# The indexer's transposes one slot sooner in a software-pipelined step, and vector's split ahead of the close

## The chip, the cores and the metric

The kernel runs on one core of one Trainium2 chip. A core has five engines that run their own instruction streams and meet at semaphores: TensorE (PE in the profile, matrix products and transposes), VectorE (DVE), ScalarE (ACT), GpSimd (POOL) and SyncE (SP, which issues the DMA transfers). The metric is the device time of one execution in microseconds (us), as the median of several.

## What is computed

One layer of a hybrid encoder: 4096 new frames of a prompt (32 tiles of 128 rows) and 128 frames of eight running streams (tile 32). Cut to what bears on the change:

```python
h = rms_norm(x, norm_g)
p = h @ w_in                  # q, k, v, gate of two head groups, and the indexer's qi, ki, wi
# group A: attention in a sliding window;  group B: for each query the 256 best keys
r = relu(einsum('bqhe,ble->bqhl', qi, ki_all))        # 4 heads of 64, all keys so far
score = einsum('bqhl,bqh->bql', r, wi)
_, idx = lax.top_k(score, 256)
# attention over those keys, gates silu(ga), silu(gb), then y @ w_out + x
```

The kernel has three stages. The first, which the change touches, projects every tile, normalizes, stores q, k, v and gates, scores each tile against all keys so far (the indexer), and finds the 256th largest score of each row by a search of 32 counting tests. The second does the attention, the last the output projection and the sample frames.

## The kernel before

Stage one is a loop over steps t = 0 to 33, each of 12 slots. In step t PE projects tile t group by group: `kv` at slot 0, `qa` at 2, `qb` at 4, `idx` at 6, and from step 10 on the gates `ga` at 8 and `gb` at 10. From step 23 on two more gates, those of the tiles 0 to 9 that were left out, follow at slots 9 and 11. PE also transposes the next tile's x (slots 5 and 7), the indexer's query and key of tile t (slot 9, `transpose_indexer`, L578 and L581 of the profile), and computes the scores of tile t-1 (L614), spread over slots 0 to 7. Each engine's stream is in program order, written out by such slots.

ACT evacuates what PE projects (L700 for most groups and, as `ring`, for gates, L698 for `idx`), copies the transposes (L722 for the indexer's query, L725 for its key, L670 for x), applies relu to the scores (L737), which POOL weighs and adds (L908 to L913). Between these ACT runs the search of even tiles (tests at L807). DVE runs the search of odd tiles (tests at L1043), squares for the norms (L946, L950), the split of the indexer's query and key into a high and a low part (L956, L961), and the close of every search (`choose`, L969 to L980; for ACT's tiles it starts at L989). A planner decides where this extra work stands between the tests: it adds up fixed costs (`dve_us`, `act_us`, `test_us`, `close_us`) and puts each piece in when its planned time `us_at(t, slot)` is reached. It orders, it does not time.

The search of a pair of tiles takes two steps. ACT's search ends in an odd step, so DVE's close of it stands in an odd step near slots 9 to 11; in most of the odd steps it stood ahead of the split. PE's first score product of the next step waits for both parts of the split (semaphore `s_lo`). The transposes use two PSUM banks in turn: the one of the indexer's key (L581) waits until ACT has copied the second half of the next x (L670, one slot after the evacuation of `idx`).

Of the kernel before, what the change touches and what calls it, by code (L numbers as in the profile page):

```python
# [23 lines left out]
P = 128  # L24
# [7 lines left out]
HD = 64  # L32
# [94 lines left out]
SLOTS = 12  # L127
RELU_GAP = 1.8
BIG = float(2 ** 100)
TESTS = 32  # L130
# [80 lines left out]
def dve_us(t, slot):  # L211

    return 3.4 * (slot == 6) + 1.2 * (slot == 11) if t <= TILES else 0.0

# [69 lines left out]
def stage_one(nc, x_prompt, x_sample, norm_g, w_in, q_norm_a, k_norm_a, q_norm_b, k_norm_b,  # L284
# [3 lines left out]
    with ExitStack() as ctx:  # L288
# [94 lines left out]
        def _(sp):  # L383
# [67 lines left out]
            for t in range(TILES + 2):  # L451
# [36 lines left out]
                else:  # L488
                    sp.dma_start(b_kidx_sample[0].rearrange("b t d -> (b t) d"), proj[:, PKI:PKI + HD]).then_inc(s_ki, 16)
                chosen_until(us_at(t, 9))  # L490
                if t >= LATER:
                    sp.wait_ge(s_ev, PROJ["ga", t] + 1)
                    from_ring(gates[t, :, 0:STEP])
                if e is not None:
                    sp.wait_ge(s_ev, PROJ["ga", e] + 1)
                    from_ring(gates[e, :, 0:STEP])
                if t == TILES:
                    sp.wait_ge(s_tc, PIECE["iq", t] + 1)
                    from_ring(qi_new, HD)
                    sp.wait_ge(s_tc, PIECE["ik", t] + 1)  # L500
                    from_ring(ki_new, HD, P)
                sp.wait_ge(s_kn, t + 1)
# [33 lines left out]
        def _(pe):  # L536
# [63 lines left out]
            def score_units(u, slot):  # L600

                for j, (c, n) in enumerate(units(u)):
                    if unit_slot(u, j) != slot:
                        continue
                    if j == 0:
                        pe.wait_ge(s_lo, 2 * u + 2)
                    for h in range(IDX_HEADS):
                        at = SCORED[u] + IDX_HEADS * j + h
                        if at >= 4:
                            pe.wait_ge(s_rl, at - 3)  # L610
                        if at == 0:
                            pe.wait_ge(s_rampc, 1)
                        for part in range(2):
                            ins = pe.matmul(s_bank[at % 4][:, 0:n], qi[:, part, h * P:(h + 1) * P], kiT[:, c:c + n],  # L614
                                            start=(part == 0), stop=(part == 1))
                        ins.then_inc(s_s, 1)
# [3 lines left out]
            for t in range(TILES + 2):  # L620
                for slot in range(SLOTS):
# [10 lines left out]
                    if slot in (5, 7) and t < TILES:  # L632
                        transpose_x((slot - 5) // 2, t + 1)
                    if slot == 9 and t <= TILES:
                        transpose_indexer(t)
# [5 lines left out]
        def _(act):  # L641
# [97 lines left out]
            def background():  # L739
# [5 lines left out]
                for t in range(TILES + 3):  # L745
                    for slot in range(SLOTS):
                        before, b = divmod(SLOTS * t + slot - 1, SLOTS)
                        yield us_at(t, slot)
                        if b == 0 and 1 <= before <= TILES + 1:
                            copy_piece("k", before - 1)  # L750
                        for at, name, of in groups_of_step(before) if 0 <= before <= TILES else ():
                            if at == b:
                                evacuate(name, of)
# [6 lines left out]
                        if slot == 4 and t < TILES:  # L760
                            square_x(t + 1)
                        if b == 9 and before <= TILES:
                            copy_piece("iq", before)
                            copy_piece("ik", before)
                        if 3 <= t <= TILES:
# [164 lines left out]
        def _(dve):  # L930
# [73 lines left out]
            def background():  # L1004

                taken = 2
                for t in range(TILES + 5):
                    for slot in (0, 3, 6, 9, 11):
                        while taken < SEARCHED and FOUND_AT[taken] <= us_at(t, slot):
                            yield FOUND_AT[taken]  # L1010
                            choose_act(taken)
                            taken += 2
                        if slot == 6 and t <= TILES:
                            yield us_at(t, slot)
                            sum_heads(t)
                        if slot == 11 and t < TILES:
                            yield us_at(t, 10.3)
                            split_q(t)
                            split_k(t)
# [1514 lines left out]
```

## Time and profile before

| | us |
|---|---|
| median of 3 runs (5093.58 to 5100.38) | 5097.78 |
| the profiled execution | 5096.76 |
| its span, first to last instruction | 5095.0 |

| engine | busy us | share of the span |
|---|---|---|
| PE | 4347.4 | 85% |
| DVE | 3499.8 | 69% |
| ACT | 3443.3 | 68% |
| POOL | 1619.9 | 32% |

The times of the trace count from the span's start. Stage one ends, and the next stage's first instructions run, at 2456 us. A wait in these views is written as engine, what it was about to write, its line, and the instruction that ended the wait. The PE clock of a stretch is given as a share of 2.4 GHz.

### The profile page before, as it was taken

Reading aid. Unit: us, or ns where it says so; the run is one execution under the profiler, and the core shown is the slowest. Engines: PE = TensorE matmul, PEld = TensorE weight load, DVE = VectorE, ACT = ScalarE, POOL = GpSimd, SP = SyncE. Lnnn points to the kernel's source line nnn. Section 1 sums busy time; section 2 is a strip of 40 time slices with the busy share of each in tenths; the row PEclk is TensorE's granted clock in tenths of the full one; section 3 lists DMA queues with packets and bytes.
Section 4 is the critical chain, followed back from the end, with each engine's and each line's share of the span. In section 5 each row is a group of like instructions: output and inputs, shape, how many; then the busy total and the mean of one; then the engine's idle time right before and its main releaser. Section 6 shows DMA issues by size and latency. Waiting matters only on the chain. (4 is left out here: it accounts for less than half of the span.)

```text
span 5095.0 us, 78325 instructions
## 1 busy us (share of the span) xinstructions
PE 4347.4 (85%) x26505; PEld 2718.1 (53%) x26505; DVE 3499.8 (69%) x6644; ACT 3443.3 (68%) x6887; POOL 1619.9 (32%) x1358
## 2 busy tenths in 40 slices
PE   6777888777677786767689999989999999989999
PEld 3344444434343343434366777767777777754444
DVE  1277779888797898989477777787777778625111
ACT  1588888888787798872488888858788885520100
POOL 1345566667557757777210000000000000000000
PEclk8888889888788898978799999999999999999999
DMA  5211111100010111101421111011010010044422
GB/s 143 70 44 45 38 39 40 37 35 28 33 42 33 37 45 38 36 32 48 157 72 58 44 51 40 28 54 41 25 42 25 28 40 26 10 126 132 117 93 103
DMA packets 201975, 276.98 MB, mean 54 GB/s; under 512 B 50496, under 2 KB 134176, under 8 KB 201056
## 3 DMA queue, kind: packets, MB, share of 16 engines
q1 hardware_dynamic: 198624, 271.81, 16.9%
q8 instruction: 220, 3.60, 0.3%
q14 instruction: 171, 1.40, 0.1%
q10 hardware_dynamic: 2960, 0.17, 0.0%
HBM read 156.73 MB, written 114.16 MB: 53 GB/s over the span
## 5 line engine op out<-in xcount | busy, mean ns | idle before, releaser
L596 PE MATMUL bank<-w,x 128*128 128x512 f32 (+1 forms) x2848 | 1258.6, 598 | 19.2 <-DVE w L941 12.8
L1043 DVE TENSOR_SCALAR_CACHE_REDUCE ties<-score,cand 128x512 int8<-128x512 f32 (+13 forms) x448 | 1110.6, 2479 | 122.1 <-POOL score L917 106.7
L596 PEld LDWEIGHTS bank<-w,x 128*128 128x128 f32 x2848 | 576.9, 206 | 608.6 <-issue 549.7
L807 ACT ACTIVATE act_junk<-score,a_cand,a_sign 128x384 int8<-128x384 f32 (+13 forms) x420 | 879.4, 2094 | 14.0
L614 PE MATMUL bank<-kiT,qi 128*128 128x512 f32 (+3 forms) x1136 | 396.5, 489 | 450.5 <-ACT relu L737 244.9
L1834 DVE CUSTOM_DVE_ANT_0 row<-bank,mask 128x512 f32<-128x512 f32 (+3 forms) x1024 | 622.6, 639 | 181.6 <-PE bank L1573 180.3
L1540 POOL TENSOR_TENSOR near_bias<-table,mask 128x2048 f32<-128x2048 f32 (+1 forms) x32 | 129.5, 4047 | 1767.8 <-DVE part L1834 1751.4
L1768 ACT ACTIVATE pT<-bank 128x512 f32<-128x512 f32 (+2 forms) x704 | 368.4, 523 | 428.5 <-PE bank L1589 426.6
L1670 ACT ACTIVATE row<-row,top 128x1024 f32<-128x1024 f32 (+7 forms) x640 | 632.9, 990 | 4.0 <-DVE top L1847 4.0
L1573 PE MATMUL bank<-kT,qb 64*128 64x256 f32 (+1 forms) x4352 | 609.6, 397 | 9.0 <-DVE part L1834 5.6
L1589 PE MATMUL bank<-ident,row 128*128 128x128 f32 x4224 | 594.6, 281 | 26.4 <-DVE pT L1945 19.6
L1945 DVE COPY pT<-bank 128x512 f32<-128x512 f32 (+2 forms) x704 | 425.2, 604 | 255.8 <-PE bank L1589 254.2
L1618 PE MATMUL bank<-pT,v 128*64 128x128 f32 x8448 | 590.0, 280 | 0.0
L913 POOL TENSOR_TENSOR score<-score,relu 128x512 f32<-128x512 f32 (+3 forms) x426 | 560.3, 1315 | 33.4
L614 PEld LDWEIGHTS bank<-kiT,qi 128*128 128x128 f32 x1136 | 237.6, 232 | 578.3 <-ACT relu L737 307.0
L1618 PEld LDWEIGHTS bank<-pT,v 128*64 128x64 f32 x8448 | 450.9, 137 | 171.1 <-issue 163.7
L910 POOL TENSOR_TENSOR relu<-relu,weight 128x512 f32<-128x512 f32 (+3 forms) x426 | 499.3, 1172 | 76.9 <-ACT relu L737 76.7
L1589 PEld LDWEIGHTS bank<-ident,row 128*128 128x128 f32 x4224 | 453.1, 141 | 132.2 <-issue 97.0
L737 ACT ACTIVATE relu<-bank 128x512 f32<-128x512 f32 (+3 forms) x568 | 297.7, 554 | 252.1 <-POOL score L913 177.0
L2290 PE MATMUL bank<-wo,mix_in 128*128 128x512 f32 x1024 | 450.9, 599 | 0.0
L1573 PEld LDWEIGHTS bank<-kT,qb 64*128 64x128 f32 x4352 | 380.3, 187 | 125.5 <-issue 72.1
L908 POOL TENSOR_TENSOR score<-relu,weight 128x512 f32<-128x512 f32 (+3 forms) x142 | 164.6, 1159 | 651.4 <-issue 527.9
(255 smaller groups left out, 4900.1 us busy)
## 6 DMA issues: line engine op xcount, KB each, us to landing
qk_t<-ring SPq DMA_DIRECT2D x66, 256.0 KB, 2.0
gates<-ring SPq DMA_DIRECT2D x66, 256.0 KB, 2.0
gate<-gates SPq DMA_DIRECT2D x33, 512.0 KB, 3.4
out<-x_in SPq DMA_DIRECT2D x33, 512.0 KB, 2.9
x<-in_x_prompt SPq DMA_DIRECT2D x32, 512.0 KB, 3.7
mixed<-mixT SPq DMA_DIRECT2D x64, 256.0 KB, 2.0
mix_in<-mixed SPq DMA_DIRECT2D x32, 512.0 KB, 4.3
x_in<-in_x_prompt SPq DMA_DIRECT2D x32, 512.0 KB, 3.8
```

The costliest lines, as they stand in the source:

```text
L596: ins = pe.matmul(p_bank[n % 2][:, 0:n1 - n0], held[:, c * P:(c + 1) * P], w[:, c, n0:n1], start=(c == 0), stop=(c == KC - 1))
L614: ins = pe.matmul(s_bank[at % 4][:, 0:n], qi[:, part, h * P:(h + 1) * P], kiT[:, c:c + n], start=(part == 0), stop=(part == 1))
L807: tick(act.activation(junk, row, ACT.Sign, bias=c, scale=back, accum_out=a_sum[:, :]))
L910: k = tick(pool.tensor_tensor(r, r, weighs, ALU.mult))
L913: pool.tensor_tensor(to, to, r, ALU.add).then_inc(s_pa, 1)
L1043: n = tick(dve.tensor_scalar(ties[:, 0:width], row, c.bitcast(F32), 0.0, ALU.is_ge, ALU.add, accum_out=counts[:, i:i + 1]))
L1573: ins = pe.matmul(s[:, h * STEP + c0:h * STEP + c0 + m], qb[t % 2][half, g, :], kT[half, c + c0:c + c0 + m], start=True, stop=True)
L1589: ins = pe.transpose(t_bank[h][:, b * P:(b + 1) * P], held, ident[:, :])
L1618: ins = pe.matmul(oT[0 if k < 2 else 1][half * HD:(half + 1) * HD, col:col + P], value, pT[h][at % 2][:, b * P:(b + 1) * P], start=first, ...
L1670: act.activation(at, at, ACT.Exp, bias=bias, accum_out=out).then_inc(s_exp, 1)
L1834: ins = dve.tensor_tensor_reduce(row[k % 2][:, h, c0:c0 + w0], s[:, h * STEP + c0 - c:h * STEP + c0 - c + w0], more, 1.0, PAD, ALU.add, AL ...
L2290: ins = pe.matmul(y_bank[k % 2], held, w[:, c, i * STEP:(i + 1) * STEP], start=(c == 0), stop=(c == KC - 1))
```

## The change

Five edits in stage one. PE's `transpose_indexer` stands at slot 8 instead of 9, and so ahead of the first gate's projection. ACT's copies of the two transposes follow one slot sooner, ahead of its evacuation of the first gate. DVE's split is planned at slot 9.3 instead of 10.3, and the planner no longer puts the close of an ACT tile at slot 9 but at 7 or 11, so that no close stands between slot 9 and the split. PE's first score product waits for the query's part of the split alone, and only the last one (whose keys hold the new tile) for the key's. SP's stores of the sample tile's query and key follow the new order once, in step 32.

```diff
+SPLIT = 9.3
 def dve_us(t, slot):
-    return 3.4 * (slot == 6) + 1.2 * (slot == 11) if t <= TILES else 0.0
+    return 3.4 * (slot == 6) + 1.2 * (slot == 9) if t <= TILES else 0.0
...
                     if j == 0:
+                        pe.wait_ge(s_lo, 2 * u + 1)
+                    if j == len(units(u)) - 1:
                         pe.wait_ge(s_lo, 2 * u + 2)
...
-                    if slot == 9 and t <= TILES:
+                    if slot == 8 and t <= TILES:
                         transpose_indexer(t)
...
+                        if b == 8 and 0 <= before <= TILES:
+                            copy_piece("iq", before)
+                            copy_piece("ik", before)
                         for at, name, of in groups_of_step(before) if 0 <= before <= TILES else ():
                             if at == b:
                                 evacuate(name, of)
...
-                        if b == 9 and before <= TILES:
-                            copy_piece("iq", before)
-                            copy_piece("ik", before)
...
-                    for slot in (0, 3, 6, 9, 11):
-                        while taken < SEARCHED and FOUND_AT[taken] <= us_at(t, slot):
+                    for slot in (0, 3, 6, 7, SPLIT, 11):
+                        while slot != SPLIT and taken < SEARCHED and FOUND_AT[taken] <= us_at(t, slot):
...
-                        if slot == 11 and t < TILES:
-                            yield us_at(t, 10.3)
+                        if slot == SPLIT and t < TILES:
+                            yield us_at(t, SPLIT)
                             split_q(t)
                             split_k(t)
```

PE's instructions at the end of step 21 of the kernel before, from the last score product of tile 20 to the first projection of step 22 (bank is PSUM, a projection is 8 products here):

```order
L614 MATMUL bank<-kiT,qi 128x128 x8
L596 MATMUL bank<-w,x 128x324 x8
L557 MATMUL bank<-ident,x 128x128 x4
L596 MATMUL bank<-w,x 128x512 x8
L578 MATMUL bank<-ident,proj 128x128 x4
L581 MATMUL bank<-ident,proj 128x128
L596 MATMUL bank<-w,x 128x512 x8
L614 MATMUL bank<-kiT,qi 128x512 x8
```

The same place in the changed kernel, whose lines stand one to three further down:

```order
L617 MATMUL bank<-kiT,qi 128x128 x8
L597 MATMUL bank<-w,x 128x324 x8
L558 MATMUL bank<-ident,x 128x128 x4
L579 MATMUL bank<-ident,proj 128x128 x4
L582 MATMUL bank<-ident,proj 128x128
L597 MATMUL bank<-w,x 128x512 x16
L617 MATMUL bank<-kiT,qi 128x512 x8
```

The five transposes of the indexer stood between the two gates and now stand ahead of both. PE's stream changes so in each of the 23 steps that have gates; before step 10 it does not change.

DVE's instructions at the end of step 21 before, around the close of tile 18 (score is its row of scores, ties and mask are results):

```order
L1043 TENSOR_SCALAR ties,counts<-score,cand 128x2560
L989 TENSOR_SCALAR pick<-a_found 128x1
L991 SCALAR_TENSOR_TENSOR pick<-a_found,pick 128x1
L993 TENSOR_SCALAR ties,pick<-score,pick 128x2432
...
L972 SCALAR_TENSOR_TENSOR score<-ties 128x2432
L975 SCALAR_TENSOR_TENSOR pick<-score,pick 128x1
L977 SCALAR_TENSOR_TENSOR ties<-score,pick,ties 128x2432
L980 SCALAR_TENSOR_TENSOR mask<-ties,mask 128x2432
L956 TENSOR_TENSOR qi<-bank,qi 128x512
L961 TENSOR_TENSOR kiT<-bank,kiT 64x128
```

The same place in the changed kernel:

```order
L1046 TENSOR_SCALAR ties,counts<-score,cand 128x2560
L959 TENSOR_TENSOR qi<-bank,qi 128x512
L964 TENSOR_TENSOR kiT<-bank,kiT 64x128
L1050 TENSOR_SCALAR flag<-counts 128x1
L1053 TENSOR_SCALAR cand<-flag,cand 128x1
L1046 TENSOR_SCALAR ties,counts<-score,cand 128x2560
L992 TENSOR_SCALAR pick<-a_found 128x1
```

The split moved from behind the close to ahead of it, over one test too. It passes a close in steps 9, 17, 19, 21, 23, 25, 27, 29 and 31, and two to four tests of a search in most others.

## Rows read from the trace of the kernel before

**Rows 1.** Busy time by stretch: steps 4 to 21, and 22 to 30

```profile
core 0: us, PE busy (x) PEld busy (x) DVE busy (x) ACT busy (x) POOL busy (x), PEclk, DMA share, GB/s
187.00:1330.00 1143.00, 868.18 (x2506) 469.23 (x2507) 900.17 (x1414) 974.03 (x1919) 675.08 (x580) 0.86 0.11 39
1330.00:2300.00 970.00, 727.74 (x1922) 380.80 (x1921) 838.93 (x736) 801.00 (x1125) 660.95 (x535) 0.85 0.11 37
```

**Rows 2.** Waits of PE, ACT, DVE, 187 to 1330 us: total, times, longest

```profile
PE bank L614 <- DVE kiT L961: 183.0, 19, 22.1
...
ACT proj L700 <- PE bank L596: 59.3, 27, 6.3
...
ACT relu L737 <- PE bank L614: 6.9, 6, 3.3
...
DVE ties L946 <- ACT proj L700: 115.0, 10, 26.0
DVE ties L1043 <- POOL score L917: 45.7, 7, 12.0
```

**Rows 3.** Waits of PE and DVE, 1330 to 2300 us

```profile
PE bank L614 <- DVE kiT L961: 7.0, 3, 3.8
...
DVE ties L1043 <- POOL score L917: 61.0, 5, 15.9
DVE ties L946 <- ACT proj L700: 42.8, 5, 12.9
```

**Rows 4.** Timeline at the end of step 21: start, length, instruction, idle before

```profile
1273.13 7.03 PE L596 MATMUL bank<-w,x 128*128 128x512 f32 x16
...
1281.95 7.03 PE L596 MATMUL bank<-w,x 128*128 128x512 f32 x16
1311.06 3.60 PE L614 MATMUL bank<-kiT,qi 128*128 128x512 f32 x8 [22.07 <-DVE kiT L961]
...
1292.33 2.75 DVE L993 TENSOR_SCALAR_CACHE_REDUCE ties<-score,pick 128x2432 int8<-128x2432 f32 x1
...
1288.87 0.67 ACT L700 ACTIVATE ring<-bank,row_scale 128x512 f32<-128x512 f32 x1
...
1312.31 0.60 ACT L737 ACTIVATE relu<-bank 128x512 f32<-128x512 f32 x1 [2.61 <-PE bank L614]
...
1321.86 0.69 ACT L700 ACTIVATE proj<-bank,row_scale 128x512 f32<-128x512 f32 x1 [6.30 <-PE bank L596]
```

**Rows 5.** Timeline at the end of step 22

```profile
1390.09 0.48 PE L581 MATMUL bank<-ident,proj 128*128 128x128 f32 x1 [6.62 <-ACT x L670]
...
1393.30 0.67 ACT L700 ACTIVATE ring<-bank,row_scale 128x512 f32<-128x512 f32 x1
```

**Rows 6.** Timeline at the end of step 26, four gates

```profile
1757.18 7.03 PE L596 MATMUL bank<-w,x 128*128 128x512 f32 x16
...
1781.42 0.48 PE L581 MATMUL bank<-ident,proj 128*128 128x128 f32 x1 [7.01 <-ACT x L670]
1781.69 8.86 PE L596 MATMUL bank<-w,x_later 128*128 128x512 f32 x16
...
1803.72 2.41 PE L614 MATMUL bank<-kiT,qi 128*128 128x512 f32 x8
...
1806.64 0.66 ACT L700 ACTIVATE ring<-bank,row_scale 128x512 f32<-128x512 f32 x1
```

**Rows 7.** Timeline in step 25: DVE's close begins, ACT's first gate

```profile
1667.68 0.21 DVE L989 TENSOR_SCALAR pick<-a_found 128x1 f32<-128x1 f32 x1
...
1675.24 0.67 ACT L700 ACTIVATE ring<-bank,row_scale 128x512 f32<-128x512 f32 x1
```

**Rows 8.** Timeline in the middle of step 22

```profile
1352.52 2.17 DVE L946 TENSOR_TENSOR ties<-proj 128x1280 f32<-128x1280 f32 x1 [12.93 <-ACT proj L700]
...
1361.61 6.22 POOL L908 TENSOR_TENSOR score<-relu,weight 128x512 f32<-128x512 f32 x1
```

**Rows 9.** Timeline at the end of step 31

```profile
2341.91 3.59 PE L614 MATMUL bank<-kiT,qi 128*128 128x512 f32 x8 [13.48 <-DVE kiT L961]
```

**Rows 10.** Busy time and PE clock in PE's wait of step 21

```profile
1290.00:1311.00 21.00, 0.00 (x0) 0.00 (x0) 20.27 (x18) 19.11 (x29) 0.00 (x0) 0.59 0.18 62
```

More of the change, by code:

```diff
@@ L490, in _ @@
                 chosen_until(us_at(t, 9))
+                if t == TILES:
+                    sp.wait_ge(s_tc, PIECE["iq", t] + 1)
+                    from_ring(qi_new, HD)
+                    sp.wait_ge(s_tc, PIECE["ik", t] + 1)
+                    from_ring(ki_new, HD, P)
                 if t >= LATER:
@@ L496, in _ @@
                     from_ring(gates[e, :, 0:STEP])
[L497 to L501, printed above, removed]
                 sp.wait_ge(s_kn, t + 1)
```

## The prediction

> **What bounds the kernel now.** I read the busy time by stretch first. Stage one ends at 2456 us of a span of 5095, and no edit touches what follows. In steps 4 to 21 ACT is busy 974 of 1143 us, DVE 900 and PE 868 [rows 1]: no engine is full, so the streams hold each other up. The waits say where. In that stretch PE waits 183.0 us in 19 places, once a step, for DVE's split ahead of the first score product. ACT waits for PE only 59.3 us at projections and 6.9 at relus; DVE waits 115.0 for the evacuation that feeds its squares and 45.7 for finished scores [rows 2]. After step 21 PE's wait for the split is gone, 7.0 us in nine steps, since four gates keep it busy, while DVE still idles 61.0 and 42.8 [rows 3]. The timeline of step 21 shows the mechanism: DVE closes ACT's tile from 1292 us on, the split comes behind the close, and PE, done with its gates at 1289.0, idles 22.07 until 1311.06. ACT reaches the first relu at 1309.7 and waits 2.61 there and 6.30 at the next projection [rows 4]. ACT's later evacuation releases DVE in step 22 after 12.93 of idling [rows 8]. So the loop runs DVE's close, split, PE, ACT, DVE, and of PE's long wait only ACT's part reaches it.
>
> **The change part by part.** No product, copy or test is added or removed; five transposes on PE, two copies on ACT and two subtractions on DVE move per step.
>
> *The split ahead of the close (gain).* At step 21 ACT's copies take the place of its gate evacuation, 1288.87 instead of about 1293. DVE stands at a test's end at 1288.5 (one test ahead of its close at about 1292), so the split is done near 1291. PE has two gates to do behind the transposes: those can't end before ACT has copied x, 1281.8, so the gates end at 1282.1 + 2 x 7.03 = 1296.2. The scores begin there, 14.9 sooner, and ACT, at 1309.7, waits for nothing: it gets back 2.61 + 6.30 = 8.9, not 22. I sum it by ACT's waits, not PE's. They are 59.3 + 6.9 = 66.2 for steps 4 to 21 [rows 2]; going through the timeline, 42 of them stand behind a split, at the first relu and the first projections, and the rest at later projections, where PE has again waited for ACT. Bounds: 8.9, the one step shown, and 66.2. I take **-42**. What hides a lateness of the split now is that ACT gets there 15 us later; should the close still come first somewhere, the step is as before.
>
> *The transposes ahead of the first gate (loss).* Before, PE did a gate while ACT evacuated `idx` and copied x. Now it waits. In step 26 the gate that ran at 1757.18 for 7.03 must follow the key's transpose, which waits for ACT until 1781.42. Four gates from 1781.9 (7.03 + 8.86 + 7.03 + 7.03) end at 1811.8 instead of 1804.2, 7.6 later. ACT's last gate evacuation stood at 1806.64 and now waits 5.1, with its search behind it [rows 6]. In step 22 the first gate ends at 1390.6 + 7.0 = 1397.6, and ACT, which comes from 1393.30 and 0.8 of copies, waits 3.5 [rows 5]. Behind the waiting ACT stand its tests, the next evacuations and relus, so POOL too. The other even steps of 10 to 20 give 0.3 to 3.3 by the same reckoning, 12 for the seven with step 22; steps 24, 26 and 28 give about 5 each, 15; in the odd steps ACT arrives after the gates' new end and the price is about nothing, hidden by its tests. Sum **+27**. Bounds: nothing, where ACT's own waits for POOL absorb it, and 7.6 in each of the 23 gate steps.
>
> *DVE ahead of ACT.* In step 25 DVE reaches the split at 1667.68, but ACT copies the query only where its first gate stood, 1675.24 [rows 7]. DVE will wait about 8 us there in front of its close, and 6 or so in 23, 27 and 29: 27 us in all. I cost it at nothing, since the next even step has DVE idling, 61.0 + 42.8 us in five steps [rows 3], and it ends those steps by ACT's and POOL's time. Without that cover it costs the 27.
>
> *The end.* In step 31 PE waits 13.48 for the split until 2341.91 [rows 9]. It was ready at 2328.4; with the first gate 7.4 later it is ready at 2335.8, and nothing waits behind it but evacuations: **-5** of the 6.1. The weaker wait at the first score product saves the key's subtraction, 0.3 a step, nothing where PE comes after it. SP's two stores change places once, with work around them: nothing.
>
> Sum: -42 + 27 - 5 = -20. Against the profiled execution, 5096.8 (its span plus 1.8), that is 5077; the median of the runs shown is 1.0 above it, so **5078**.
>
> PE's clock: while PE idled from 1290 to 1311 its granted clock was 0.59 on average, so it fell to the lower level, 1.2 GHz; the gate that followed a pause in step 26 took 8.86 against 7.03 [rows 6, 10]. The Trainium skill ("TensorE: Matmul & The Clock Gate", Part 1) says the same of an idle PE, and it speaks against new pauses ahead of a gate. By it and these rows, six odd steps with a new pause lose 1.8 each, 11 in all, and the sum would be -9, 5089, if no slack took it; by the rows of step 21 alone, where ACT comes 13 us after PE, it is -20. I keep -20.
>
> **The rivals.**
>
> *PE's whole gain is passed on.* At step 21 PE gains 14.9 where ACT gains 8.9. If POOL and the relus behind start as much earlier as PE does, the 42 grows by that ratio to 70, and the sum is -70 + 27 - 5: 5050. For it: DVE has 160.7 us of idling to give in these steps [rows 2]. Against: ACT's relus stand at planned places between tests, and it doesn't idle there. Chance 0.16.
>
> *The gain is given back on the way.* ACT comes sooner to the same relus, but POOL adds no faster under DVE's closes: at 1361.61 one product took 6.22 us under DVE's scan [rows 8]. If half of the 42 ends so, -21 + 27 - 5 = +1: 5099. The change then does in effect nothing. Chance 0.22. The Trainium skill ("SBUF — State Buffer", Who interferes with whom) has GpSimd and VectorE share a pair of ports by an exclusive lock; the 6.22 agrees. By that rule each close that now meets additions stops them, and this rival gains; at step 21 the close would end at about 1309, just before ACT's relu, so it would stop none.
>
> *Slower: PE's pause ahead of the first gate runs through.* If ACT has no slack, an even step of 10 to 22 loses 3.5 (as 22 does) and one of 23 to 30 loses 5 (as 26 does): 24 + 40 = 64 against 47 gained, +17: 5115. It decides from 47 us on, 3.1 a step over these fifteen. For it: in steps 23 to 30 PE had no wait for the split left to win, so only the loss is there. Against: in odd steps ACT comes late. Chance 0.20.
>
> **How the numbers follow.** My forecast, -20 with its own range 5063 to 5089, gets 0.42. 0.2% is 10 us, about what can be told from no change here. Faster by more: the forecast's 0.42 and the first rival's 0.16, so 0.58; same 0.22; slower 0.20. The range leaves out about half of each outer rival: 5045 to 5112. It holds the bounds of the loss at 0 (5051) and most of the gain's.
>
> **What would show it.** Right: PE's waits for the split in steps 3 to 21 fall from 183 to under 50, and ACT's waits for PE at the first projections with them, by some 40; new waits appear on PE at the transposes of the indexer and ACT gets waits at `ring`; DVE gets waits of 6 to 8 us at the split in steps 23 to 29 and idles less in even steps. Steps 4 to 21 take 30 to 40 us less, steps 22 to 30 are 10 to 20 longer. Wrong: if steps 4 to 21 shrink by as much as PE's waits, ACT's plan was no limit; if the later steps grow by over 40, the pause runs through; if DVE's wait at the split lengthens odd steps, its idling was no cover.

## The result and the profile after

The changed kernel takes 5119.80 us (median of 5 runs, 5116.71 to 5121.0) against 5094.48 for the kernel before on the same chip: ratio 1.0049, 95% interval 1.0037 to 1.0061, 25 us slower. The forecast was 5078 and its range ended at 5112. The kernel before took between 5094.5 and 5095.5 on each of the chips used below, so the medians of the runs can be compared with each other. The profiled execution's span is 5114.9 us.

Busy time by stretch, answering to [rows 1]: core, stretch, then busy us of PE, PEld, DVE, ACT and POOL, the granted clock, DMA.

```profile
core 0: us, PE busy (x) PEld busy (x) DVE busy (x) ACT busy (x) POOL busy (x), PEclk, DMA share, GB/s
187.00:1330.00 1143.00, 895.03 (x2506) 476.12 (x2504) 888.38 (x1402) 973.35 (x1914) 679.99 (x577) 0.87 0.11 39
1330.00:2300.00 970.00, 704.88 (x1867) 370.01 (x1866) 814.33 (x726) 784.14 (x1102) 637.12 (x515) 0.83 0.11 37
```

Up to 1330 us ACT and POOL have done what they had before; from 1330 to 2300 every engine does less: ACT 784.1 instead of 801.0, PE 704.9 instead of 727.7. The granted clock there went from 0.85 to 0.83. The waits of the changed kernel from 187 to 1330 us, answering to [rows 2] (total, times, longest):

```profile
PE bank L617 <- ACT relu L740: 106.0, 50, 5.2
PE bank L579 <- ACT proj L701: 58.1, 19, 13.0
DVE qi L959 <- ACT qi L725: 56.8, 12, 10.2
PE bank L617 <- DVE qi L959: 41.1, 8, 13.1
PE bank L582 <- ACT x L673: 35.1, 12, 4.0
ACT proj L703 <- PE bank L597: 30.6, 14, 5.0
ACT ring L703 <- PE bank L597: 22.2, 8, 4.4
```

and from 1330 to 2300 us:

```profile
PE bank L579 <- ACT proj L701: 60.3, 7, 19.8
DVE qi L959 <- ACT qi L725: 51.1, 9, 9.2
PE bank L582 <- ACT x L673: 36.5, 8, 7.4
DVE ties L949 <- ACT proj L703: 23.0, 4, 11.1
ACT ring L703 <- PE bank L597: 21.4, 9, 5.6
```

The gain arrived: PE's wait for the split fell from 183.0 to 44.5 us (41.1 for the query's part, 3.4 for the key's) and ACT's at projections from 59.3 to 30.6. So did its counterpart. From 187 to 2300 us PE waits 118.4 us in 26 places for the evacuation of `idx` (L579) and 71.6 in 20 for the copy of x (L582). In the kernel before these were:

```profile
PE bank L581 <- ACT x L670: 48.6, 13, 7.4
PE bank L578 <- ACT proj L698: 35.5, 13, 11.5
```

ACT now waits 43.6 us in 17 places at `ring`, where the kernel before has no wait in these steps. At the end of step 22 these are the rows of PE and ACT (start, length, instruction, idle before), answering to [rows 5]:

```profile
1386.56 1.09 PE L579 MATMUL bank<-ident,proj 128*128 128x128 f32 x4 [6.19 <-ACT proj L701]
1393.81 0.48 PE L582 MATMUL bank<-ident,proj 128*128 128x128 f32 x1 [6.16 <-ACT x L673]
1394.07 16.08 PE L597 MATMUL bank<-w,x 128*128 128x512 f32 x32
...
1397.49 0.27 ACT L728 ACTIVATE kiT<-bank 128x128 fp32r<-128x128 f32 x1
1403.39 0.69 ACT L703 ACTIVATE ring<-bank,row_scale 128x512 f32<-128x512 f32 x1 [5.63 <-PE bank L597]
```

PE waits 6.19 and 6.16 us ahead of its first gate. The first gate of the two then runs from 1394.07 to 1403.29, 9.21 us instead of 7.03, and ACT waits 5.63 for it. The same stretch by windows:

```profile
1380.00:1394.00 14.00, 1.66 (x9) 1.05 (x8) 3.15 (x2) 11.99 (x19) 13.20 (x16) 0.67 0.14 51
1394.00:1404.00 10.00, 10.00 (x20) 4.31 (x20) 6.14 (x9) 4.34 (x7) 2.56 (x2) 0.78 0.00 0
1404.00:1410.00 6.00, 6.00 (x16) 2.65 (x15) 5.79 (x9) 5.83 (x8) 0.00 (x0) 1.00 0.19 66
```

The granted clock is 0.67 in the pause, 0.78 in the first gate and 1.00 in the second. Cut finer, it is 0.50 from 1390 to 1398 us and 1.00 from 1399 on: the gate begins at the lower level, 1.2 GHz. Taken in the same way from the trace, first product to last, the first gate takes 8.75 us in the mean of steps 10 to 28 (7.03 to 9.76), where before it took 7.03 in each of them. Before, it was the second gate that stood behind a pause: it took 8.26 to 9.01 us in eight of these steps, and takes 7.03 now.

To see where the time goes I follow one event, the start of ACT's evacuation of `idx` (L701) in each step, against the same event before (us, minus is sooner). The other columns are runs described below.

| step | changed | gate first | transposes alone | pauses filled |
|---|---|---|---|---|
| 10 | -9.3 | -8.4 | 1.9 | -12.2 |
| 16 | 5.7 | -11.0 | 15.6 | -5.2 |
| 19 | 9.5 | -16.1 | 22.6 | -6.4 |
| 22 | 3.7 | -27.9 | 22.3 | -18.0 |
| 23 | 9.3 | -29.4 | 26.5 | -14.5 |
| 26 | 16.2 | -27.8 | 33.0 | -8.3 |
| 30 | 27.5 | -26.5 | 46.4 | 0.1 |

The changed kernel leads by 9.3 us at step 10, where the steps get their gates, and loses most of the time from there on. Up to step 10 the changed kernel and the one with the pauses filled run the same instructions, and their columns differ by 2.9 us there: a difference of that size between two traces says nothing.

### The profile page after: what moved, and what is told of

Read it like the earlier page. It is cut to its first block and busy times, and to the rows that moved or that the text cites. A ratio compares the mean times of both kernels' runs of the same rounds, so it can differ in the third digit from the quotient of the medians.

```text
span 5114.9 us, 78353 instructions
## 1 busy us (share of the span) xinstructions
PE 4360.2 (85%) x26505; PEld 2720.6 (53%) x26505; DVE 3492.5 (68%) x6644; ACT 3445.5 (67%) x6887; POOL 1628.1 (32%) x1358
## 5 line engine op out<-in xcount | busy, mean ns | idle before, releaser
L597 PE MATMUL bank<-w,x 128*128 128x512 f32 (+1 forms) x2848 | 1284.7, 609 | 30.9 <-ACT ring L703 17.5
L597 PEld LDWEIGHTS bank<-w,x 128*128 128x128 f32 x2848 | 592.5, 212 | 642.8 <-issue 574.1
L1592 PE MATMUL bank<-ident,row 128*128 128x128 f32 x4224 | 593.6, 281 | 26.5 <-DVE pT L1948 20.0
L916 POOL TENSOR_TENSOR score<-score,relu 128x512 f32<-128x512 f32 (+3 forms) x426 | 572.1, 1343 | 33.4
L1576 PEld LDWEIGHTS bank<-kT,qb 64*128 64x128 f32 x4352 | 379.3, 187 | 125.0 <-issue 71.6
```

What stands on the lines that cost most here:

```text
L597: ins = pe.matmul(p_bank[n % 2][:, 0:n1 - n0], held[:, c * P:(c + 1) * P], w[:, c, n0:n1], start=(c == 0), stop=(c == KC - 1))
L916: pool.tensor_tensor(to, to, r, ALU.add).then_inc(s_pa, 1)
L1576: ins = pe.matmul(s[:, h * STEP + c0:h * STEP + c0 + m], qb[t % 2][half, g, :], kT[half, c + c0:c + c0 + m], start=True, stop=True)
L1592: ins = pe.transpose(t_bank[h][:, b * P:(b + 1) * P], held, ident[:, :])
```

## The experiments

Theory G: PE's pause ahead of the first gate reaches ACT and costs more than figured. Rival S: the sooner split, with DVE waiting for ACT ahead of its close, costs in the late steps.

**Gate first.** The changed kernel, but from step 10 on PE does the first gate ahead of the transposes again. ACT and DVE stay as changed.

```diff
-                    if slot == 8 and t <= TILES:
+                    if slot == 8 and t < LATER:
                         transpose_indexer(t)
                     for at, name, of in groups_of_step(t) if t <= TILES else ():
                         if at == slot and slot > 0:
                             project(name, of, of != t)
+                    if slot == 8 and LATER <= t <= TILES:
+                        transpose_indexer(t)
```

> The changed kernel, but from step 10 on PE does the first gate ahead of the indexer's transposes again; ACT's and DVE's order stay changed. Theory G (PE's pause ahead of the gate, while ACT evacuates idx and copies x, is what costs the time): PE's waits at the transposes fall from 118 us to about 70, ACT's waits at ring vanish, and the time falls by 35 to 50 against the changed kernel, to about 5075. Theory S (DVE, which now comes to the split ahead of ACT's copy, waits there in front of its close, and this costs the time): these waits stay, and so does the time, 5115 to 5120.

Measured: 5061.50 us (5058.55 to 5069.2), ratio 0.9933 (0.9921 to 0.9945), against 5119.80 with the pause: the one move costs 58 us and hides a gain of 34. G holds. S isn't answered by that alone, since DVE's waits at the split in steps 23, 25, 27 and 29 fell too, from 8.7, 9.2, 6.3 and 8.2 us to 2.0, 5.7, 3.0 and 3.5. But by the event these four steps bring only 3.3 us of the difference, and steps 24, 26 and 28, in which DVE waits as long in both runs, bring 12.0. So S doesn't hold either for the late steps. Its waits from 187 to 2300 us:

```profile
DVE qi L961 <- ACT qi L727: 86.6, 19, 10.2
PE bank L617 <- DVE qi L961: 63.5, 11, 13.1
PE bank L582 <- ACT x L675: 48.9, 14, 7.4
PE bank L579 <- ACT proj L703: 40.1, 13, 11.5
ACT ring L705 <- PE bank L597: 11.9, 2, 6.2
```

PE's wait at the query's transposes is 40.1 instead of 118.4. ACT's 11.9 at `ring` all stand in step 31, where the kernel before has them too; in steps 10 to 30, with 43.6 us in the changed kernel, there is none. DVE still waits 86.6 us at the split. The end of its step 22:

```profile
1362.22 0.48 PE L582 MATMUL bank<-ident,proj 128*128 128x128 f32 x1 [6.61 <-ACT x L675]
1362.49 8.38 PE L597 MATMUL bank<-w,x 128*128 128x512 f32 x16
...
1366.07 0.69 ACT L705 ACTIVATE ring<-bank,row_scale 128x512 f32<-128x512 f32 x1
```

PE's wait for x is still there, and a gate behind it still takes 8.38, but it is the second gate, for which ACT comes only at 1380.52. ACT finds the first one ready.

**The transposes alone**, on the kernel before, without ACT's, DVE's and the planner's edits:

```diff
-                    if slot == 9 and t <= TILES:
+                    if slot == 8 and t <= TILES:
                         transpose_indexer(t)
```

> The kernel before with PE's edit alone: the indexer's transposes ahead of the first gate. ACT's copies and DVE's split stay where they were. Theory G: all of the loss without the gain, 20 to 45 us slower than before, 5115 to 5140. Theory S: no change, 5095, since DVE's order is untouched.

Measured: 5143.23 us (5139.78 to 5145.17), ratio 1.0089 (1.0076 to 1.0103): 48 us slower. By the event above, the even steps 10 to 22 lose 31.1 together and the odd ones between them win 6.5; from 23 on, steps 24, 26 and 28 lose 14.6, the odd ones 5.3, and step 30 gives 0.9 back. The waits from 187 to 2300 us:

```profile
PE bank L578 <- ACT proj L698: 123.7, 26, 18.3
PE bank L581 <- ACT x L670: 71.1, 20, 7.4
ACT ring L700 <- PE bank L596: 54.3, 18, 5.5
...
ACT L700 <- PE bank L596: 5.2, 1, 5.2
```

The last row is the first gate of step 10, in front of which ACT loads a table, so that it has no tile's name. ACT's new waits for first gates are so 59.5 us, more than the loss. A gain stands against them: with the transposes sooner, PE's wait for the split is 119.6 us instead of 190.0, and from step 10 to 30 ACT's waits for PE are 15.1 us less at projections and 7.6 less at relus. The 48 us are what is left of a larger loss.

**The rule on the close alone**, on the kernel before: no close of an ACT tile at slot 9, the split still planned at 10.3, but never behind a close.

```diff
+SPLIT = 10.3
...
-                    for slot in (0, 3, 6, 9, 11):
-                        while taken < SEARCHED and FOUND_AT[taken] <= us_at(t, slot):
+                    for slot in (0, 3, 6, 7, SPLIT, 11):
+                        while slot != SPLIT and taken < SEARCHED and FOUND_AT[taken] <= us_at(t, slot):
...
-                        if slot == 11 and t < TILES:
-                            yield us_at(t, 10.3)
+                        if slot == SPLIT and t < TILES:
+                            yield us_at(t, SPLIT)
```

> The kernel before with the planner's edit alone: the split stays planned at 10.3, but no close of an ACT tile is put in at slot 9. PE's and ACT's order stay as before, so DVE comes to the split no sooner than ACT's copy. Theory G and theory S both expect a gain here, since neither the pause nor DVE's wait is made: PE's waits for the split fall by about half of 183 us in the steps up to 21, and the time by 10 to 25, to 5070 to 5085. The rival that the gain is given back downstream expects 5095.

Measured: 5100.48 us (5096.94 to 5104.03), ratio 1.0008 (0.9999 to 1.0017). A miss: no gain. The trace has a lead of 12.6 us at PE's first score product behind step 23, and is 0.4 behind at the same place of step 26. DVE's row in step 25 says what is new there:

```profile
1676.42 0.69 DVE L957 TENSOR_TENSOR qi<-bank,qi 128x512 fp32r<-128x512 f32 x1 [17.89 <-ACT qi L723]
```

DVE had finished its test at 1658.5 and held its close back for 17.89 us, since ACT's copies still stood behind the gate here. In steps 23, 27 and 29 it is 14.8, 15.3 and 18.8. The next run takes these waits away.

**The same rule in steps 0 to 22 only**, as an edit of the run before.

```diff
-                    for slot in (0, 3, 6, 7, SPLIT, 11):
-                        while slot != SPLIT and taken < SEARCHED and FOUND_AT[taken] <= us_at(t, slot):
+                    for slot in (0, 3, 6, 7, 10.3, 11) if t < LATER_FROM else (0, 3, 6, 9, 11):
+                        while slot != 10.3 and taken < SEARCHED and FOUND_AT[taken] <= us_at(t, slot):
...
-                        if slot == SPLIT and t < TILES:
+                        if slot == (10.3 if t < LATER_FROM else 11) and t < TILES:
```

> The kernel before with the planner's rule on the split (vector's split planned ahead of the close, no close at slot 9) in steps 0 to 22 only; the transposes and the steps from 23 on stay as before. If the rule did its work up to step 23 (the first score product came 12.6 us sooner there) and the long waits of vector at the split in steps 23 to 29 (15 to 19 us each) ate it afterwards, the lead of 10 to 13 us stays to the end: 5081 to 5086 us. If the lead is lost in the late steps for a reason of their own, whatever vector does at the split there: 5093 to 5097. If the rule by itself is worth nothing where the transposes are not sooner: 5095 with no lead at step 23 either.

Measured: 5081.24 us (5079.66 to 5086.84), ratio 0.9975 (0.9966 to 0.9985). The lead at the end of step 23 was 11.4 and at 31 it is 12.3. So the rule is worth some 14 us by itself up to step 22, and costs 19 from step 23 on. By the event, steps 23, 25, 27 and 29, in which DVE waits 15 to 19 us in front of its close, lose 20.9, the even steps between them 0.9, and step 31 gives 6.7 back. That the waits are the cause is argued from where the time is lost, not shown by a run of its own.

**The whole change in steps 0 to 9 only**, where no step has gates: transposes, copies, rule and split sooner there, the rest as before. Of the diff the planner's `dve_us` is left out.

```diff
-                    if slot == 9 and t <= TILES:
+                    if slot == (8 if t < LATER else 9) and t <= TILES:
                         transpose_indexer(t)
...
-                        if b == 9 and before <= TILES:
+                        if b == (8 if before < LATER else 9) and 0 <= before <= TILES:
...
-                    for slot in (0, 3, 6, 9, 11):
-                        while taken < SEARCHED and FOUND_AT[taken] <= us_at(t, slot):
+                    for slot in (0, 3, 6, 7, 9.3, 11) if t < LATER else (0, 3, 6, 9, 11):
+                        while slot != 9.3 and taken < SEARCHED and FOUND_AT[taken] <= us_at(t, slot):
...
-                        if slot == 11 and t < TILES:
-                            yield us_at(t, 10.3)
+                        if slot == (9.3 if t < LATER else 11) and t < TILES:
+                            yield us_at(t, 9.3 if t < LATER else 10.3)
```

> The change in steps 0 to 9 alone, where there are no gates; from step 10 on the kernel before. In the changed kernel the scores of step 9 began 14.4 us sooner than before. Theory G: this gain is kept, 8 to 14 us faster than before, 5081 to 5087, since the loss begins with the gates. Theory S: about the same number, a little less for the few DVE waits at the split in steps 3 to 9. If the early gain is absorbed by later idling, 5095.

Measured: 5084.85 us (5080.43 to 5089.82), ratio 0.9978 (0.9968 to 0.9988). From 187 to 500 us ACT's waits at projections fall from 25.6 to 16.5 while PE's at the split fall from 63.9 to 43.2: 9.1 less on ACT, and the event leads by 9.0 to 9.3 from step 14 to the end. The gain is ACT's part of the wait, as the prediction had it. The moved transposes can cost nothing here, since without a gate PE's order stays the same.

**The close ahead again**: gate first, but a close may stand at slot 9, ahead of the split at 9.3.

```diff
-                    for slot in (0, 3, 6, 7, SPLIT, 11):
+                    for slot in (0, 3, 6, 9, SPLIT, 11):
```

> e1_gate_first (5061.5), but a close may again be put in at slot 9, ahead of the split at 9.3: one slot sooner is kept, the rule on the close is undone. If the close ahead of the split is what holds PE in odd steps up to 21, most of e1's gain there goes: PE's waits for the split rise from 67 to over 110 us and the time to 5075 to 5085. If one slot sooner is the whole gain (e3_close_behind alone gave nothing), it stays within 5 us of 5061.

Measured: 5085.49 us (5083.61 to 5089.25), ratio 0.9981 (0.9973 to 0.999). PE's waits at the split are 112.5 us in 16 places, the longest 19.1. The rule is worth 24 of the 34 us that gate first wins.

**The pause in the late steps alone**: gate first in steps 10 to 22, the transposes ahead of the gate from 23 on.

```diff
-                    if slot == 8 and t < LATER:
+                    if slot == 8 and (t < LATER or LATER_FROM <= t <= TILES):
                         transpose_indexer(t)
...
-                    if slot == 8 and LATER <= t <= TILES:
+                    if slot == 8 and LATER <= t < LATER_FROM:
                         transpose_indexer(t)
```

> e1_gate_first, but in steps 23 to 32 the transposes are ahead of the first gate, as in the changed kernel; in steps 10 to 22 the gate comes first. Theory G: in the changed kernel the scores fell from 7.2 to 31.6 us behind between steps 22 and 30, and e1 held its lead there, so this one loses 20 to 25 us of e1's lead: 5080 to 5087. If the loss is only one of the steps with two gates, it stays at 5061.

Measured: 5080.80 us (5074.61 to 5085.26), ratio 0.9971 (0.996 to 0.9982). Against gate first that is 19 for the steps from 23 on, and so, as the difference, 39 of the 58 for steps 10 to 22. By the event in its trace it is 14 for the steps from 23 on.

**The split later**: gate first with another planned time for the split.

```diff
-SPLIT = 9.3
+SPLIT = 9.8
```

> e1_gate_first with DVE's split planned at slot 9.8 instead of 9.3, so that DVE waits less often for ACT's copy (it waits 86.6 us at the split in e1). Theory S: DVE's wait in front of its work costs time, so fewer waits give 3 to 10 us, 5052 to 5058. Theory G (the wait is covered by DVE's later idling, PE's path alone counts): no gain, 5060 to 5068, since the split is only later.

Measured: 5064.01 us (5062.76 to 5066.96), ratio 0.9939 (0.9927 to 0.9952). DVE's waits at the split fall from 86.6 to 61.4 us and the time doesn't (5061.50 before that), while PE's wait for the split stays near what it was, 65.7 after 63.5. In steps 23, 25, 27 and 29 DVE's waits even rise, to between 5.4 and 6.9 us, and the run loses nothing there. Waits of this size in front of the close are covered.

**The pause in the odd steps alone**: gate first in the even steps from 10 on, the transposes first in the odd ones.

```diff
-                    if slot == 8 and t < LATER:
+                    if slot == 8 and (t < LATER or t % 2 and t <= TILES):
                         transpose_indexer(t)
...
-                    if slot == 8 and LATER <= t <= TILES:
+                    if slot == 8 and LATER <= t <= TILES and t % 2 == 0:
                         transpose_indexer(t)
```

> The version with the first gate ahead of the transposes (5061.5 us), but in the odd steps from 11 on the transposes go first, as in the changed kernel. Step by step in the traces, the position of the scalar engine's evacuation of the index heads fell back, between this version and the changed kernel, by 46 us in the even steps from 10 on and by 9 in the odd ones; with the transposes alone on the kernel before it was 45 and -1. If a pause in an odd step is nearly free, because the scalar engine comes later than the gates' end there: 5058 to 5072. If the pause costs in every step alike, about 2.5: 5085 to 5095.

Measured: 5075.57 us (5066.73 to 5077.07), ratio 0.9957 (0.9944 to 0.9969), just above the first theory's 5058 to 5072. By the medians the odd steps cost 14 of the 58 and the even ones, as the difference, 44. The event in its trace gives 8 for the odd steps.

**A shorter pause**: the changed kernel, with ACT's copy of the second half of x right ahead of its evacuation of `idx` instead of a slot behind it. PE then waits once ahead of the first gate, not twice.

```diff
+                        if b == 6 and before < TILES:
+                            copy_x(1, before + 1)
                         for at, name, of in groups_of_step(before) if 0 <= before <= TILES else ():
                             if at == b:
                                 evacuate(name, of)
...
-                        if b in (5, 7) and before < TILES:
-                            copy_x((b - 5) // 2, before + 1)
+                        if b == 5 and before < TILES:
+                            copy_x(0, before + 1)
```

> The changed kernel (5119.8), but ACT copies the second half of the next x right ahead of its evacuation of idx, one slot sooner, so that the key's transpose no longer waits for it. Theory G: the pause ahead of the first gate shortens by a slot (PE waits 71.6 us at that transpose in the changed kernel), and the time falls by 15 to 35, to 5085 to 5105. If the pause's length is not what costs, 5120.

Measured: 5083.66 us (5081.21 to 5087.95), ratio 0.9978 (0.9969 to 0.9987): 36 us come back. Its waits from 187 to 2300 us:

```profile
PE bank L579 <- ACT proj L701: 139.0, 29, 18.6
...
ACT x L673 <- PE bank L558: 20.0, 9, 4.0
...
ACT ring L703 <- PE bank L597: 8.6, 7, 3.3
```

The 71.6 us of PE's second wait (L582) are gone, and ACT's at `ring` fell from 43.6 to 8.6; 20.0 us of new waits for the x transposes are the price. The first gate is still slow behind the one pause, 8.43 us in the mean of steps 10 to 28, but it starts sooner, and ACT seldom comes before its end.

**Both mends**, gate first and the shorter pause together.

> The changed kernel with both mends: from step 10 on the tensor engine does the first gate ahead of the transposes, and the scalar engine copies the second half of x right ahead of the copy out of the index heads' product. If the tensor engine's pause ahead of the first gate is the whole price, it is mostly gone with the first mend, and the second adds little: 5055 to 5062 us, the same as with the first mend alone (5061.5) or up to 6 better. If the copy put sooner only moves the wait to the scalar engine (20.0 us of waits for the x transposes in its own run) and nothing is left to win by it: 5065 to 5080.

Measured: 5069.27 us (5068.43 to 5074.11), ratio 0.9952 (0.9938 to 0.9966). Worse than gate first alone by 8, where the same edit won 36 with the pause ahead of the first gate. That was the expectation's second case. ACT has 21.8 us of waits at x here, and PE's waits for the split are 85.7 us instead of 63.5; how the 8 comes out of them isn't shown.

**The pauses filled.** Is it the end of the pause that costs, or also the clock behind it? Two runs add products whose results the first gate overwrites. They are extra work on PE, so the time can fall only by way of the clock.

```diff
+            def fill(t, count):
+                if t < LATER:
+                    return
+                n = PROJ["ga", t]
+                pe.wait_ge(s_ev, n - 1)
+                for _ in range(count):
+                    pe.matmul(p_bank[n % 2][:, 0:STEP], x[t % 2][:, 0:P], w[:, 0, 0:STEP], start=True, stop=True)
...
                 to = piece_bank("iq", t)
+                fill(t, 6)
                 pe.wait_ge(s_ev, PROJ["idx", t] + 1)
...
+                fill(t, 0 if t % 2 else 5)
                 to = piece_bank("ik", t)
```

> The changed kernel with idle products put into the tensor engine's two new pauses, into the bank of the first gate, which overwrites them: six products of 128x512 ahead of the indexer's transposes of the query and, in even steps, five ahead of that of the key, from step 10 on. In the changed kernel the first gate behind the pauses takes 8.7 us in the mean, against 7.0 to 7.3 before. If the lower granted clock behind the pause is a part of the price, as the theory has it that the even steps' cost was figured with a gate of 7.0, the first gate goes back to 7.0 to 7.5 us, the scalar engine's waits at ring fall from 43.6 us to under 30, and 15 to 25 us come back: 5095 to 5105. If only the time at which the pause ends counts, the gates may run faster but the time stays: 5115 to 5125. If the products outlast the pauses in many steps, they cost by themselves: over 5125.

Measured: 5127.64 us (5125.56 to 5130.66), ratio 1.0063 (1.005 to 1.0077). The first gate took 7.03 in 18 of the 21 steps 10 to 30, but in 10 of them PE then waited for nothing at either transpose: the products outlasted the pauses. Gain and cost can't be told apart, so the next run takes a count for each step from the pauses' measured lengths, one product per 0.9 us.

```diff
+FILL = {10: (5, 3), 12: (4, 4), 13: (6, 0), 14: (1, 2), 15: (3, 0), 16: (1, 2), 17: (3, 0), 18: (1, 2), 19: (3, 2),
+        20: (12, 2), 21: (4, 3), 22: (6, 6), 23: (4, 0), 24: (7, 3), 25: (2, 0), 26: (16, 7), 27: (4, 0), 28: (19, 7),
+        29: (7, 0), 30: (5, 0)}
...
-                fill(t, 6)
+                fill(t, FILL.get(t, (0, 0))[0])
...
-                fill(t, 0 if t % 2 else 5)
+                fill(t, FILL.get(t, (0, 0))[1])
```

> The changed kernel with idle products in the pauses ahead of the first gate again, but their number set step by step from the measured length of each pause (one 128x512 product for each 0.9 us, none where the pause is under 1 us), so that they end about with the pause. In the run with a fixed number the gates were at 7.0 us but the products outlasted most pauses, and the two effects could not be told apart. If the lower granted clock behind a pause is a part of the price, as the gates take 8.7 us in the changed kernel and 7.0 to 7.3 without a pause: the scalar engine's waits at ring fall under 35 us and 10 to 25 us come back, 5095 to 5110. If the clock counts for nothing and only the end of the pause does: 5115 to 5125.

Measured: 5098.71 us (5094.12 to 5104.26), ratio 1.0006 (0.9997 to 1.0015): 21 us less than the changed kernel, with more work on PE. Its busy time by stretch, and its waits from 187 to 2300 us:

```profile
187.00:1330.00 1143.00, 949.52 (x2665) 501.51 (x2666) 907.43 (x1426) 990.15 (x1944) 694.13 (x592) 0.89 0.11 40
1330.00:2300.00 970.00, 774.83 (x2075) 402.10 (x2073) 824.73 (x724) 787.52 (x1100) 646.06 (x524) 0.89 0.11 36
```

```profile
PE bank L591 <- ACT proj L714: 29.8, 20, 5.8
PE bank L595 <- ACT x L686: 24.6, 16, 3.6
ACT ring L716 <- PE bank L610: 22.0, 14, 4.4
```

The granted clock is 0.89 where it was 0.83 from 1330 us on, the first gate takes 7.29 us in the mean of steps 10 to 30 (7.03 or 7.04 in 18 of 21) where the changed kernel has 8.73, and ACT's waits at `ring` are half. At the end of its step 22:

```profile
1364.76 0.66 PE L591 MATMUL bank<-ident,proj 128*128 128x128 f32 x4 [1.94 <-ACT proj L714]
1365.25 5.32 PE L584 MATMUL bank<-w,x 128*128 128x512 f32 x12
1372.09 0.33 PE L595 MATMUL bank<-ident,proj 128*128 128x128 f32 x1 [1.53 <-ACT x L686]
1372.26 13.90 PE L610 MATMUL bank<-w,x 128*128 128x512 f32 x32
...
1379.39 0.69 ACT L716 ACTIVATE ring<-bank,row_scale 128x512 f32<-128x512 f32 x1 [3.34 <-PE bank L610]
```

L584 are fillings, L610 the two gates, 13.90 us instead of 16.08. ACT waits 3.34 for the first one, where the changed kernel had 5.63.

## Why the prediction was wrong, point by point

**The step that failed: "The transposes ahead of the first gate (loss) ... Sum +27".** It measured +48 alone, with a gain of its own in it, and +58 within the change. The direction and the route (PE's pause, ACT's wait at its gate, the search behind it) were right, and so was the place but for the odd steps; the term was half of what it is, since it left out the slower gate behind the pause and the odd steps. By stretches, from the event:

| | figured | transposes alone | in the change |
|---|---|---|---|
| even steps 10 to 22 | 12 | 31.1 | 34.3 |
| odd steps 11 to 21 | 0 | -6.5 | 5.3 |
| steps 23 on | 15 | 19 | 15 by the event, 19 by its own run |

The two right columns are the event's shifts, step by step, against the kernel before and against gate first. The sum from step 10 to 31 in the change is 55; the medians give 58, and the two profiled executions, spans of 5114.9 and 5067.4, 47.5. A few us of these columns are no more certain than that.

The route can be counted too. These are ACT's waits for PE at gates in steps 10 to 30 (`ring`, and the first gate of step 10), of which gate first has none:

| | figured | in the change | pauses filled |
|---|---|---|---|
| even steps 10 to 22 | 12 | 26.1 | 11.6 |
| odd steps 11 to 29 | 0 | 9.8 | 3.6 |
| even steps 24 to 30 | 15 | 12.9 | 9.3 |

They make up 48.8 of the 55 us; the largest of the rest is 6.5 us of relus that wait for POOL.

**What stood in place of it.** In the steps from 23 on I took the gates' lengths from step 26, where one already followed a pause and took 8.86. In the even steps 10 to 22 I set the first gate at 7.03 as it was before, "the first gate ends at 1390.6 + 7.0 = 1397.6, and ACT ... waits 3.5". It follows the pause now and took 9.21; 3.5 + 2.2 is 5.7, and ACT waited 5.63. With the pauses filled and the gate back at 7.03 it waited 3.34. With the pauses filled, the event falls back against gate first by 18.6 us over steps 10 to 22, where the changed kernel falls back by 39.6, and by 11.8 from there to step 30, where the changed one does by 15.4. So the clock took its share where it had been left out of the sum, and what is left, 30.5, is near the figured 27; ACT's waits at gates, 24.4, are under it. The medians of the run with measured fillings put 21 of the 58 us on the clock. It can be more, since in some steps the fillings may have outlasted the pause and cost by themselves. That the rest comes from the pause itself is shown by gate first and by the shorter pause; by medians it is 37, 10 over what was figured, by the two traces 26 to 30, and how it splits over steps is only as good as one trace each.

The text of the prediction had this. It weighed the gate behind a pause, 8.86 against 7.03, and the rule of the Trainium skill ("TensorE: Matmul & The Clock Gate", Part 1) that an idle PE falls to the lower clock. It priced it for six odd steps alone, 11 us, and then kept the sum without it. It belonged in the seven even steps, where ACT waits for that gate: 7 x 1.8 = 13 more by its own rows, and a sum of -7. ACT's waits at gates in these steps fell by 14.5 with the pauses filled. The granted clock of 0.78 in the gate of step 22 agrees with the rule; that its price is paid where another engine waits for the product, and is nothing where the second gate bears it (gate first), is what the runs add.

**"In the odd steps ... the price is about nothing"**: in the change they cost 14 us by the medians, 8 by the event. Alone they cost nothing in sum (-6.5 and 5.3), but not for the reason given, that ACT arrives after the gates' new end: ACT waits 15.1 us at `ring` in steps 11 to 29 there, more than the 9.8 in the change. In the odd steps 11 to 21 its waits for PE at projections and relus fell by 18.0 at the same time and hid them. In the change the split's part of the edits takes such waits away by itself, and nothing is left there to hide the loss.

**The split ahead of the close, -42.** Gate first has it all, and by the event leads 27.9 at step 22; the whole is worth 34. So -28 for -42, and the rest, 6.1 by the event, is gained in step 31, where -5 was figured. The method, to sum ACT's waits and not PE's, held: ACT's at projections fell by 28.7 (59.3 to 30.6, 31.2 in gate first), PE's at the split by 138.5. Its waits at relus fell from 6.9 to 1.7 in gate first and those at the evacuation of the indexer's weights rose from 10.1 to 14.3, 29.1 less in all. Only the count of which waits stand behind a split was too high: 42 of 66.2, where 33.3 went and 4.2 came back elsewhere. The rival of the whole gain passed on, 70, is out.

**DVE ahead of ACT, costed at nothing.** Right at the size it had: DVE waited 8.7, 9.2, 6.3 and 8.2 us in steps 23, 25, 27 and 29, and these steps, pause and all, cost 3.3 us against gate first. Not right in general: where the waits were 15 to 19 us, with the close behind, the same four steps cost 20.9.

**The gain given back on the way** didn't happen: with gate first the lead of 27.9 us at step 22 is 26.5 at step 30.

**The slower rival**, that the pause runs through, is what came, near its 5115, and its point of decision held (58 is over 47). Its working was the same reckoning without ACT's slack, 24 + 40; the runs give 39 + 19. So it came near by a sum of two errors.

**What would show it.** PE's split waits under 50, new waits at the transposes and at `ring`, DVE's of 6 to 9 at the split: all seen. ACT's waits at projections fell by 28.7 where some 40 were looked for. Steps 4 to 21 were to shrink by 30 to 40; by the event they came out 3.5 longer. Steps 22 to 30 were to grow by 10 to 20 and grew by 22. "Over 40" in the later steps, as the sign of a pause that runs through, looked for it in the wrong half.

**The best version** of those run is gate first: PE's order from step 10 on as before, and the four other edits, 5061.50 us, 0.7% faster than before.

## What to carry to other kernels

When an operation is moved ahead of work that used to cover its wait, price the work behind it at the clock that it will meet after the pause, and ask for each product who waits for it: the same slow gate cost nothing as the second and 2 us a step as the first. Price the parts of a change on the kernel that the other parts leave, not each on the one before: here two parts took the same waits away, which made one of them look cheaper by itself (48 us) than it was (58). And split a change on the chip by engine and by stretch of steps before judging it: here four other edits, worth 34 us together, stood behind one that cost 58.

## What was not expected of the hardware

The kernel got faster by giving PE useless work: 21 us with fillings of one product per 0.9 us of pause, and the granted clock from 0.85 to 0.89 from 187 to 2300 us. With fillings too long, the gates were as fast and the time was 8 us over that of the changed kernel. The two edits on x and on the gates don't add up either: -36 where the pause stands ahead of the first gate, +8 where it doesn't.
